# Late modulation blocks: fetched by GpSimd's queue instead of SyncE's queue

## The reference: what is computed

```
ada = (c @ w_ada + b_ada)[:, None, :]               # c: (1, 1024), w_ada: (1024, 6144)
shift1, scale1, gate1, shift2, scale2, gate2 = split(ada, 6)
h    = rmsnorm(x, g_norm1) * (1 + scale1) + shift1
proj = h @ w_in                                     # q, k, v, gates of two attention branches
y_fox = forgetting_attention(...)                   # 8 heads of 64
y_dsa = indexer_sparse_attention(...)               # 8 heads, top 64 keys of each query
x = x + gate1 * (merged @ w_out)
h2 = rmsnorm(x, g_norm2) * (1 + scale2) + shift2
x = x + gate2 * (square(relu(h2 @ w_mlp1)) @ w_mlp2)
```

## Time and profile before

| What | Value |
|---|---|
| median of three runs | 1083.36 us |
| the profiled execution, its own time | 1082.66 us |
| its span in the profile | 1080.9 us |
| PE busy | 1041.5 us (96%) |
| PE weight load busy | 1011.9 us (94%) |
| DVE busy | 649.0 us (60%) |
| ACT busy | 546.4 us (51%) |
| POOL busy | 362.9 us (34%) |
| DMA, all on hardware queues | 197.37 MB, mean 183 GB/s |
| chain that ended last | PE 84%, DVE 7%, ACT 3%, DMA 2%, POOL 2% |

### The profile page before, as it was taken

How to read it: one execution, slowest core, us unless ns; L and a number is a source line. 1 busy time by engine, 2 the same in 40 slices (tenths; PEclk the granted TensorE clock), 3 DMA queues, 4 the chain that set the end, 5 groups by cost and what they waited for, 6 DMA issues and landing times.

```text
span 1080.9 us, 19685 instructions
## 1 busy us (share of the span) xinstructions
PE 1041.5 (96%) x8492; PEld 1011.9 (94%) x8492; DVE 649.0 (60%) x834; ACT 546.4 (51%) x768; POOL 362.9 (34%) x192
## 2 busy tenths in 40 slices
PE   2999999999999999999999999999999989999998
PEld 1699999999999999999999999999898889999998
DVE  5867668666765654637865454445857756444444
ACT  2477767744656444564345344343754545444441
POOL 4028368330545433450302342221433212242231
PEclk9999999999999999999999999999999999999999
DMA  9988587536576655533546555566533145555531
GB/s 329 303 266 254 174 286 237 192 118 197 183 257 222 196 177 174 195 117 118 171 152 210 172 194 179 172 202 198 148 110 109 49 147 178 192 181 191 177 136 40
DMA packets 169859, 197.37 MB, mean 183 GB/s; under 512 B 5379, under 2 KB 137900, under 8 KB 169644
## 3 DMA queue, kind: packets, MB, share of 16 engines
q1 hardware_dynamic: 169772, 196.11, 56.1%
HBM read 195.03 MB, written 1.06 MB: 181 GB/s over the span
## 4 chain that ended last, share of the span: by engine, by line
PE 84%; DVE 7%; ACT 3%; DMA 2%; POOL 2%; issue 1%; SPq 0%; DVEq 0%; ACTq 0%; POOLq 0%
PE bank L516 83%; DVE w_lo L1856 3%; DMA ada_raw<-in_w_ada 1%; ACT w_hi L1277 1%; DMA xT<-in_x 1%; ACT ada_raw L1267 1%; PE bank L759 1%; POOL big L1716 0%; ACT h_hi L1371 0%; DVE big L2321 0%; DVE head_bias L2409 0%; DVE fresh L2184 0%; DVE big L2310 0%; POOL qk L1716 0%; POOL probs L1716 0%
## 5 line engine op out<-in xcount | busy, mean ns | idle before, releaser
L1856 DVE TENSOR_TENSOR w_lo<-w_raw,w_hi 128x2048 fp32r<-128x2048 f32 x158 | 389.5, 2469 | 244.5 <-ACT w_hi L1277 243.5
L516 PE MATMUL bank<-h_hi,w_hi 128*128 128x256 f32 x1328 | 371.6, 287 | 5.2 <-DVE w_lo L1856 2.4
L1277 ACT ACTIVATE w_hi<-w_raw 128x2048 fp32r<-128x2048 f32 x158 | 301.4, 1909 | 139.4 <-PE bank L516 132.3
L516 PE MATMUL bank<-h_hi,w_lo 128*128 128x256 f32 x1328 | 366.4, 283 | 0.0
L516 PE MATMUL bank<-h_lo,w_hi 128*128 128x256 f32 x1328 | 345.3, 283 | 0.0
L516 PE MATMUL bank<-u_hi,w_hi 128*128 128x256 f32 x1040 | 294.1, 286 | 4.4 <-DVE w_lo L1856 2.0
L516 PE MATMUL bank<-u_hi,w_lo 128*128 128x256 f32 x1040 | 291.6, 284 | 0.0
L516 PE MATMUL bank<-u_lo,w_hi 128*128 128x256 f32 x1040 | 282.5, 284 | 0.0
L1671 POOL TENSOR_TENSOR u_lo<-fresh,u_hi 128x512 fp32r<-128x512 f32 x60 | 142.4, 2375 | 416.3 <-ACT u_hi L1286 416.2
L516 PEld LDWEIGHTS bank<-h_hi,w_hi 128*128 128x128 f32 x1328 | 253.5, 192 | 11.3 <-issue 6.9
L516 PEld LDWEIGHTS bank<-h_hi,w_lo 128*128 128x128 f32 x1328 | 253.6, 192 | 0.0
(11 more groups left out here) (264 smaller groups left out, 962.8 us busy)
## 6 DMA issues: line engine op xcount, KB each, us to landing
w_raw<-in_w_mlp SPq DMA_DIRECT2D x32, 1024.0 KB, 5.4
w_raw<-in_w_up SPq DMA_DIRECT2D x32, 1024.0 KB, 5.4
w_raw<-in_w_down SPq DMA_DIRECT2D x32, 1024.0 KB, 5.0
w_raw<-in_w_in SPq DMA_DIRECT2D x21, 1024.0 KB, 6.5
ada_raw<-in_w_ada SPq DMA_DIRECT2D x19, 1024.0 KB, 7.8
w_raw<-in_a_w_in SPq DMA_DIRECT2D x10, 1024.0 KB, 5.1
w_raw<-in_w_o SPq DMA_DIRECT2D x8, 1024.0 KB, 5.1
w_raw<-in_w_out SPq DMA_DIRECT2D x4, 1024.0 KB, 5.1
```

The costliest lines, as they stand in the source:

```text
L516: return pe.matmul(dst, lhsT, rhs, start=start, stop=stop, skip_group_check=True)
L1277: act.activation(w_hi[:, n % PARTS_RING, :], w_raw[:, slot_of[n], :], ACT.Copy).then_inc(hi_w, 1)
L1856: dve.tensor_tensor(w_lo[:, n % PARTS_RING, :], w_raw[:, slot_of[n], :], w_hi[:, n % PARTS_RING, :].bitcast(F32), ALU.subtract).then_inc(l ...
```

## The change

SP's list keeps only late blocks 8 and 9. The other fourteen, 10 to 23, are issued by POOL: directly behind its last add of block a it waits for that add's own semaphore and issues the DMA of block a + 2 into the half just freed. These DMAs signal a new pair of semaphores, `ada_more`, since a semaphore is used by one queue alone, and ACT waits on these for blocks 10 and up. Nothing else moves: the same bytes go to the same places, and the instructions on data keep their order on each engine.

```diff
@@ plan_loads
     for n in range(4, N_UNITS):
         order.append(("w", n))
-        if n - LOAD_LAG in ADA_LATE:
+        if ADA_LATE.get(n - LOAD_LAG, ADA_UNITS) < ADA_FIRST + 2:
             order.append(("a", ADA_LATE[n - LOAD_LAG]))
@@ two_blocks
         ada_full = [sem(f"ada_full{s}") for s in range(2)]
+        ada_more = [sem(f"ada_more{s}") for s in range(2)]
@@ ada_in
             else:
-                engine.wait_ge(ada_full[a % 2], 16 * ((a - ADA_FIRST) // 2 + 1))
+                if a < ADA_FIRST + 2:
+                    engine.wait_ge(ada_full[a % 2], 16)
+                else:
+                    engine.wait_ge(ada_more[a % 2], 16 * ((a - ADA_FIRST) // 2))
@@ SyncE, load_ada
                 elif a in (8, 9):
                     sp.wait_ge(ada_vector, {8: 6, 9: 2}[a])
-                elif a > 9:
-                    sp.wait_ge(ada_part_sum, pool_turn(a - 2) + 1)
@@ GpSimd, ada_unit
                 pool.tensor_tensor(ada_late[:, turn % 2, :], tiles[:, 0, :], tiles[:, 1, :], ALU.add).then_inc(ada_part_sum, 1)
+                if a + 2 < ADA_UNITS:
+                    cols = w["w_ada"].rearrange("(k p) n -> p k n", p=P)[:, :, 256 * (a + 2):256 * (a + 2) + 256]
+                    pool.wait_ge(ada_part_sum, turn + 1)
+                    pool.dma_start(ada_tiles(a + 2), cols).then_inc(ada_more[a % 2], 16)
```

## The result

The changed kernel took 1087.62 us (median of 20 runs, 1086.22 to 1089.35), the kernel before 1083.47 us beside it (20 runs, 1082.95 to 1089.38). The ratio is 1.0032, 95% interval 1.0024 to 1.0041: **slower by 3.5 us**. (The interval is 2.6 to 4.4 us; the two medians as they stand lie 4.15 us apart.) The profiled execution took 1089.17 us with a span of 1087.4; before it was 1082.66 and 1080.9, so 6.5 us lie between the two profiles.

What follows compares the result with a forecast made beforehand. PE was taken as the bound, busy 1011.45 of 1031.00 us from 50 us on. Terms -1.0 (block 21) and +2.7 (block 17) gave +1.7 us, median 1083.36 to 1085.1 us; range 1081.8 to 1098.0.

Steps and rivals of the forecast that it cites:

- the likeliest case: The forecast itself, 1085.1 us, chance 0.35; its own range 1082.4 to 1086.5 us, from a stall of 0 to 4.1.
- SP's freed queue is worth 0: SP's waits on POOL go, weights load up to 11.7 us earlier; ACT never waits for them, so 0.
- -1.0 us for block 21: Block 21 is fetched earlier, ending ACT's 4.68 us wait and PE's 1.03 us gap at 309.81: -1.0 us.
- G = 3 us: G, the time one DMA issue holds POOL's list, taken as 3 us, nearer to a pass over a tile.
- The landing, 0.7 us later: A block issued by POOL lands 6.2 us after issue, against 5.5 by SP, as pieces move only once written.
- The remainder before 164.27 is covered: 0: DVE's remainder after block 15: POOL's bias pass moves by 6 us, covering the block's 0.9 us delay; 0, otherwise +0.9.
- +2.7 us at block 17: Two POOL issues delay block 17, landing 4.4 us later; PE stalls before step 0's product in the sparse attention: +2.7 us.
- One: Rival: POOL's issue as cheap as SP's, G of 0.4 to 1.5, only block 21's gain left; 1082.4 us, chance 0.25.
- Two: Rival: POOL's issues wait for DVE's remainders, at 146.6 and 157.7, each 2.3 us longer; 1089.7 us, chance 0.15.
- Three: Rival: issue as long as the adds, G about 6, in POOL's unbroken stretch from 146.62; 1095.9 us, chance 0.15.
- Four: Rival: all 4.6 us that PE waits for remainders (`w_lo`) go away; 1078.8 us, chance 0.06.

Runs made afterwards that it cites:

- Experiment 12: Changed kernel with blocks 15, 16 and 17 fetched by SP, POOL issuing the other eleven: 1082.85 us, ratio 0.9991 [0.9979, 1.0002].
- experiment 4: Kernel before with blocks 20 to 23 earlier in SP's list, no issue on POOL: 1083.85 us, ratio 0.9990 [0.9977, 1.0002].
- 11: Kernel before with blocks 20 to 23 earlier in SP's list, timed a second time: 1082.86 us, ratio 0.9989 [0.9981, 0.9998].
- 7: Changed kernel with block 15 fetched by SP, POOL held by four writes in place of that issue: 1086.98 us, ratio 1.0031.
- 10: Kernel before, SP fetching all blocks, plus one 128x8 DMA issued by POOL right ahead of the two biases: 1090.35 us, ratio 1.0060.
- 1: Kernel before, POOL held by a wait and four writes where it would issue, SP fetching all blocks: 1085.58 us, ratio 1.0002.
- 5: Kernel before with POOL held by four writes where it would issue, but only two behind block 14: 1084.95 us, ratio 1.0007.
- 6: Changed kernel with four writes on POOL behind the issue of block 16: 1088.35 us, ratio 1.0037.
- 9: Changed kernel with one 128x8 write and its wait on POOL behind the issue of block 16: 1088.07 us, ratio 1.0034.
- 8: Changed kernel with block 16 alone fetched by SP and no hold in its place: 1086.41 us, ratio 1.0023.
- 2: Changed kernel with POOL waiting before the two biases until DVE has written the remainder of unit 17: 1095.36 us, ratio 1.0089.

## Why the prediction came out as it did

**The time and its sign.** 1087.6 us is inside the range of 1081.8 to 1098.0, and slower (0.50) was a little likelier than the same (0.44). But it is above the likeliest case's own range, which ended at 1086.5, and the way to it was another than the forecast's.

**That SP's freed queue is worth 0: right.** The wait moved from POOL to DVE (936.9 us against 875.4 + 49.1) and ACT still waits for no weight. Experiment 12 shows it from the other side: eleven blocks off SP's queue, and no more gained than experiment 4 gains with none.

**-1.0 us for block 21: right.** -1.25 in the profile, 1.1 to 1.2 by experiments 4 and 11.

**G = 3 us: wrong, it is 1.2.** The line of all fourteen issues in the changed kernel (ns min, median, max):

```profile
L1712 POOL DMA_DIRECT2D ada_raw<-in_w_ada x14: 902/902/1081, 76.8 to 315.4; - x14
```

I had argued that 1024 pieces are nearer to a pass over a tile than to the shortest instruction of 0.71 us. They were not. The 0.30 us ahead of it is the wait on POOL's own add, which I had put at nothing.

**The landing, 0.7 us later: right for block 15, wrong for others.** Block 15 took 5.82 us where SP's took 5.34 (issued 146.69, there at 152.03 before), 0.5 us more. The Trainium skill (DMA: Bandwidth & Descriptors, "Latency and other measured facts") has 0.4 us between the two paths for the first byte; this one block is near it. But blocks 11 to 13 took 7.4 to 7.8 us where SP's took 5.3 to 5.4, and block 17 took 9.02 where SP's took 5.47. SP put a weight behind each of blocks 11 to 13, and that weight then took 7.9 to 9.2 us; in the changed kernel the weight goes out 0.86 us ahead of the block and takes 5.3. So about 2 us moved from the weight to the block. That the two share the transfers, and the first to go out is served first, fits these numbers and was not tested by itself. It cost PE nothing here: ACT's waits at blocks 11 and 13 grew from 0.28 to 1.75 us and from 0.59 to 1.84, and no gap of PE followed.

**"The remainder before 164.27 is covered: 0": this step failed.** I had seen that this remainder ran beside POOL's wide bias, and I let the biases move by 6 us and so out of its way. With G at 1.2 they moved by 2.6 us (157.74 against 155.15) and DVE's request by 2.1. In both figures are the 1.30 us by which this execution ran late from the start; without them it is 1.3 and 0.8. So the request came 0.4 us before the end of the first bias and no longer 0.15 us behind it, and the meeting went another way. The term that I had set to 0, with +0.9 as the price of being wrong, was +3.61, and +1.31 of clock behind it. What showed the cause: a DMA issue right ahead of the two biases, in experiments 7 and 10 (10.14 and 9.66 us) as in the changed kernel (9.40), against 3.59 us or less wherever writes with waits stood between or in the issue's place (experiments 1, 5, 6, 9). A small table of the long remainder, all from traces:

| kernel | right ahead of the first bias | request in | us | served |
|---|---|---|---|---|
| before | last add of block 14 | second bias | 6.54 | behind it |
| 8 | last add of block 14 | second bias | 5.90 | behind it |
| 1 | writes | first bias | 3.10 | behind it |
| 5 | writes | first bias | 2.66 | behind it |
| 6 | issue, four writes | first bias | 3.59 | behind it |
| 9 | issue, one write | first bias | 2.67 | behind it |
| after | issue of block 16 | first bias | 9.40 | two instructions later |
| 7 | issue of block 16 | first bias | 10.14 | two instructions later |
| 10 | issue of 128x8 | first bias | 9.66 | two instructions later |

No kernel has its request in the first bias with a plain add ahead of it. Other places in the traces fill that hole. The first three rows are from the kernel before, the last two from the changed kernel:

```profile
468.76 0.75 POOL L1719 TENSOR_TENSOR ada_late<-probs 128x256 f32<-128x256 f32 x1
469.47 1.29 POOL L1716 TENSOR_TENSOR big<-big 128x512 f32<-128x512 f32 x1
...
469.71 3.19 DVE L1856 TENSOR_TENSOR w_lo<-w_raw,w_hi 128x2048 fp32r<-128x2048 f32 x1 [5.96 <-ACT w_hi L1277]
...
134.31 2.40 POOL L1705 TENSOR_TENSOR ada_raw<-ada_raw 128x1024 f32<-128x1024 f32 x1
...
135.84 3.03 DVE L1862 TENSOR_TENSOR w_lo<-w_raw,w_hi 128x2048 fp32r<-128x2048 f32 x1 [2.24 <-ACT w_hi L1279]
```

At 469.71 the request falls into the first of two adds in a row of which neither has to wait (the second runs from 470.71), with a plain add right ahead of them. It is served behind that first one. At 135.84 it falls into the add right behind an issue (133.39 to 134.29), but the next add waits for its predecessor's result. It too is served behind the add that it met. The fourteen traces hold 274 remainders of more than 2.6 us, and all but three are served directly behind the instruction of POOL that they met. Among those are 39 with a plain instruction ahead and no wait behind, 13 with an issue ahead and a wait behind, and 4 with a write ahead and no wait behind. The three that were passed over, by three instructions each, are the only ones with an issue ahead and no wait behind, and they waited until POOL itself came to a wait, 0.08 us ahead of the second add of block 15. So it takes both, the issue and the unbroken row behind it. All three lie at the same two biases, so how far this carries to other instructions, and what happens inside POOL, stays open.

**+2.7 us at block 17: a real mechanism, in the wrong kernel.** In the changed kernel the product of step 0 came at 188.58 with no gap. The attention had started 6.2 us late because of the gap ahead of it, and the block landed in that shadow. Nor was block 17 issued late: at 173.33, without the 1.30 us of the start 0.5 us earlier than before and not 3.7 later, as POOL's adds ran faster while the remainder stood (5.68 us for the first two of block 15 against 7.77). It then took 9.02 us to land. Where POOL was held and the first gap was not there, the second appeared at the forecast place: 1.09 us (1), 0.47 (5), 3.03 (6), 2.37 (9), 8.08 (2). Experiment 9 is nearest to the forecast's world: a short remainder, 2.37 us against the 2.7 forecast, and the clock on top. That the size came so near is in part luck: counted from the start of the program, block 17 was issued 1.9 us later there than before, not 3.7, and the attention began 0.45 us earlier, which made the gap longer.

| kernel | attention starts | block 17 at ACT | distance | gap at the product |
|---|---|---|---|---|
| before | 171.06 | 178.05 | 6.99 | 0 |
| 5 | 171.31 | 179.41 | 8.10 | 0.47 |
| 1 | 169.32 | 178.05 | 8.73 | 1.09 |
| 9 | 169.86 | 179.88 | 10.02 | 2.37 |
| 6 | 169.34 | 180.03 | 10.69 | 3.03 |
| 2 | 170.16 | 185.90 | 15.74 | 8.08 |

From 8.10 on the gap grows one for one with the distance: 7.64 us more distance from experiment 5 to 2, 7.61 us more gap. (Experiment 8, at 9.47, has its idle time in two pieces, 1.61 us in all.) This is why no edit on POOL's side gained anything. With 1.2 us free from 145 to 172, what POOL loses there shows up either as a late remainder or as a late block 17.

**The rivals.** One had the cheap issue and the wrong end: at G = 1.2 it said 1082.4. Two had the right place, remainders against POOL from 146 on, and the wrong direction: the issues did not wait for DVE (902 ns at the median; the four that fell beside a remainder took 1081, 902, 902 and 924, so at most 0.2 us more), DVE waited for what stood behind an issue. The Trainium skill (SBUF — State Buffer, "Who interferes with whom") says that a DVE instruction with two SBUF inputs contends with a GpSimd instruction that reads SBUF and not with one that only writes it, and that the order of issue decides who waits. The traces agree in the first: every remainder, which reads two tiles, that ran beside none of POOL's `tensor_tensor` instructions took 2.27 to 2.30 us, beside its writes too. In the second they agree for 271 of the 274 above. For the other three the order was as in experiment 1, a request of DVE inside the first bias, and the remainders took 9.40 to 10.14 us and not 3.10; the order of the two alone doesn't decide it. Three is out, since G is not 6. Four is out: PE's waits for `w_lo` grew.

**The clock.** I had left it out of the sum, and it made 1.3 of the 3.7 us. Gaps of 3.4 to 8 us were each followed by a low granted clock (0.50 after the changed kernel's 3.89 and around the end of experiment 2's 8.08, 0.69 around experiment 10's 3.37). After 3.03 us, in the one profile of experiment 6, the product of step 0 took 1.52 us and not 2.43 as in experiment 9 with its 2.37. So the size of the gap alone doesn't settle it; what does stays open.

## What to carry to other kernels

Before work is moved to an engine's list, read how full that list is in the stretch where it lands, and who asks for the same reads there; three of fourteen identical issues made the whole loss, in 27 us in which POOL had 1.2 us to spare. Look at the waits of the consumer first: weights that nobody waits for gain nothing from a queue of their own, and what the one late block cost, 1.1 to 1.2 us, was won back by an earlier place in SP's list (ratio 0.9989 [0.9981, 0.9998]), below the kernel before and the changed one. And where removing a gap leaves the time as it was, look for the second chain that it had covered.

## What the runs showed of the hardware that I had not expected

- A DMA issue on GpSimd is short: 0.90 us for 1 MB in rows of 1 KB, 0.74 us for 128x8 elements. The longest of the fourteen took 1.08 us.
- With a DMA issue directly ahead of a row of adds without waits on GpSimd, a subtraction on DVE that was asked for during the first of them took 9.4 to 10.1 us, against 2.7 to 3.6 us with a write of 0.12 us or more, and the wait for it, between. A kernel with one such issue of 128x8 elements ran 6.5 us longer (ratio 1.0060 [1.0045, 1.0074]). In its trace 4.6 us lie at this place.
- A block of 1 MB that went out 0.86 us behind a weight of 1 MB landed in 7.4 to 7.8 us, and in 5.3 to 5.4 when it went out 0.4 us ahead of one (blocks 11 to 13).
- The blocks moved 14.68 MB in 3808 packets on GpSimd's queue, 3.9 KB each. On SP's queue the packets fell from 169772 to 155212 while it lost the same 14.68 MB, which is 1.0 KB each.
